# A router of column groups, a shorter routing chain, and ScalarE copying the whole expert output

## The reference

```
scores = sigmoid(x @ router_w)                      # 640 x 16
best group of 4 by the sum of its top 2 of (scores + router_b)
idx    = top 2 experts inside that group;  wts = scores[idx] / sum
rows are sorted by expert, each expert padded to blocks of 128 rows
yb[block] = (silu(xb @ w_gate[e]) * (xb @ w_up[e])) @ w_down[e]
y[token]  = sum over its two rows of wts * yb
```

## Time and profile before

| | us |
|---|---|
| median of 3 runs | 2377.22 |
| lowest and highest of them | 2376.87, 2381.79 |
| profiled execution: time | 2377.54 |
| profiled execution: span from first to last instruction | 2375.8 |

### The profile page before, as it was taken

One profiled execution on the slowest core, in us unless ns is written; L12 is line 12 of the kernel. 1 busy time (PEld: TensorE's weight loads), 2 busy tenths in 40 slices (PEclk: granted clock), 3 DMA queues, 4 the chain that ended last, 5 costly groups with the idle time before them and its releaser, 6 DMA issues. The chain is left out here.

```text
span 2375.8 us, 25720 instructions
## 1 busy us (share of the span) xinstructions
PE 2062.0 (87%) x8680; PEld 1425.4 (60%) x8680; DVE 1159.2 (49%) x1677; ACT 910.7 (38%) x1290; POOL 112.1 (5%) x130
## 2 busy tenths in 40 slices
PE   6869899998479999838999999999999838999974
PEld 2335454454258878727756765874775427788853
DVE  1132323224469999754232423323232248999965
ACT  1021312212368888632211221222221127888853
POOL 0000000000010000011000100100000010000001
PEclk7669999799789999968999999999999968999986
DMA  9967010000689999461211220320210258999933
GB/s 374 409 219 314 22 37 18 19 18 6 241 288 399 399 399 399 175 245 36 80 62 39 75 79 21 101 79 27 71 36 16 77 224 303 398 399 398 399 127 123
DMA packets 169029, 424.88 MB, mean 179 GB/s; under 512 B 10621, under 2 KB 22426, under 8 KB 168986
## 3 DMA queue, kind: packets, MB, share of 16 engines
q1 hardware_dynamic: 152624, 365.52, 41.6%
q0 software_dynamic: 10944, 39.85, 4.5%
q10 hardware_dynamic: 5418, 18.96, 2.0%
HBM read 369.09 MB, written 55.21 MB: 179 GB/s over the span
## 5 line engine op out<-in xcount | busy, mean ns | idle before, releaser
L1768 DVE TENSOR_TENSOR moe_w_lo<-weight_ring,moe_w_hi 128x1024 fp32r<-128x1024 f32 x432 | 520.9, 1222 | 84.5 <-ACT moe_w_hi L1699 71.2
L1699 ACT ACTIVATE moe_w_hi<-weight_ring 128x1024 fp32r<-128x1024 f32 x432 | 456.3, 1060 | 194.3 <-PE ps L1631 125.5
L1631 PE MATMUL ps<-moe_w_hi,moe_rows_t_hi 128*128 128x512 f32 x576 | 232.8, 404 | 5.1 <-DVE moe_rows_t_lo L1773 4.7
L1229 DVE TENSOR_TENSOR ret_w_lo<-weight_ring,ret_w_hi 128x512 fp32r<-128x512 f32 x128 | 95.8, 749 | 286.1 <-ACT ret_w_hi L1165 286.1
L1631 PE MATMUL ps<-moe_w_hi,moe_rows_t_lo 128*128 128x512 f32 x576 | 226.8, 394 | 0.0
L1631 PE MATMUL ps<-moe_w_lo,moe_rows_t_hi 128*128 128x512 f32 x576 | 226.5, 393 | 0.0
L1165 ACT ACTIVATE ret_w_hi<-weight_ring 128x512 fp32r<-128x512 f32 x128 | 80.6, 633 | 309.2 <-PE ps L1042 309.2
L1042 PE MATMUL ps<-ret_w_hi,h_hi 128*128 128x512 f32 x480 | 194.0, 404 | 3.4 <-ACT weight_ring L1169 2.1
L1042 PE MATMUL ps<-ret_w_hi,h_lo 128*128 128x512 f32 x480 | 189.6, 395 | 0.0
L1042 PE MATMUL ps<-ret_w_lo,h_hi 128*128 128x512 f32 x480 | 189.6, 395 | 0.0
L1631 PEld LDWEIGHTS ps<-moe_w_hi,moe_rows_t_hi 128*128 128x128 f32 x576 | 109.3, 190 | 27.7 <-DVE moe_rows_t_lo L1773 5.5
(11 more groups left out here) (283 smaller groups left out, 2967.7 us busy)
## 6 DMA issues: line engine op xcount, KB each, us to landing
weight_ring<-in_moe_w_gate SPq DMA_DIRECT2D x36, 2048.0 KB, 12.7
weight_ring<-in_moe_w_up SPq DMA_DIRECT2D x36, 2048.0 KB, 13.8
weight_ring<-in_moe_w_down SPq DMA_DIRECT2D x36, 2048.0 KB, 12.7
weight_ring<-in_ada_w SPq DMA_DIRECT2D x24, 2048.0 KB, 23.9
weight_ring<-in_ret_w_in SPq DMA_DIRECT2D x12, 2048.0 KB, 8.7
h_normed<-rows_in POOLq DMA_DIRECT2D x36, 512.0 KB, 7.0
rows_out<-h_normed ACTq DMA_DIRECT2D x36, 512.0 KB, 6.2
rows_in<-zero_rows SPq DMA_DIRECT2D x26, 512.0 KB, 7.7
```

Source lines behind the costliest of these rows:

```text
L1229: dve.tensor_tensor(wlo[:, n % BUF, :], win[s][:, k, :], whi[:, n % BUF, :].bitcast(F32), ALU.subtract).then_inc(w_lo, 1)
L1631: mm = pe.matmul(out, lhs, rhs, start=(first and x == 0), stop=(last and x == 2))
L1699: nc.scalar.activation(whi[:, x, :], part(u, w + x), ACT.Identity).then_inc(w_hi, 1)
L1768: dve.tensor_tensor(wlo[:, x, :], part(blk[1], w + x), whi[:, x, :].bitcast(F32), ALU.subtract).then_inc(w_lo, 1)
```

## The change

- Constants: `pick` is 16 columns wide, three small tables go; the router's weights stand in tiles of 32 columns, cleared by POOL at the start, and SP waits for that ahead of their load.
- `norm` gets the router's matmuls, four slices of the width side by side in four groups of 32 output columns; the first half runs when 8 of the 16 shifts are done, the second after the last. `route` sums the four groups with `pick`.
- The routing chain has fewer operations, some of them larger; counts come as a sixth block of the ranks. PE turns two groups of rows ahead of the logits, and has six banks for it.
- In `retention` a mask comes from a table that is there already.
- In `experts` ACT copies both banks of the output, DVE none, and DVE runs `make_hidden` ahead of the last gate split.

```diff
 # norm, PE:
+for q in range(2 if router else 0):
+    pe.wait_ge(shifted, before16 + 8 * (q + 1))
+    for r, (a, n, j) in enumerate(RANGES):
+        for k in range(4):
+            mm = pe.matmul(ps[CG * k:CG * (k + 1), 2 + r, 0:n], c.router[:, 4 * q + k, :],
+                           c.h[:, 4 * q + k, a:a + n], start=(q == 0), stop=(q == 1))
 # setup, SP and POOL:
+sp.wait_ge(cleared, 1)
-sp.dma_start(c.router[:, :, :], ops["router_w"]...)
+sp.dma_start(c.router[:, :, 0:NE], ops["router_w"]...)
+pool.memset(c.router[:, :, :], 0.0).then_inc(cleared, 1)
 # route, PE:
-for r, (a, n, _) in enumerate(RANGES):
-    for k in range(KD):
-        mm = pe.matmul(ps[0:NE, 6 + r, 0:n], c.router[:, k, :], c.h[:, k, a:a + n], ...)
-pe.wait_ge(copied, 2)
-for t in range(NT):
-    mm = pe.transpose(ps[:, 0, t * NE:(t + 1) * NE], logits_t[:, t * P:(t + 1) * P], ...)
 for g in range(2 * NT):
+    if g == 2:
+        pe.wait_ge(copied, 2)
+        for t in range(NT):
+            mm = pe.matmul(ps[:, 6, t * NE:(t + 1) * NE], by_expert[:, t * P:(t + 1) * P], c.base["pick"], ...)
+        mm.then_inc(logits, 1)
     ...  # turn the rows, as before
-pe.matmul(ps[:, 1, 0:NT * NE], c.base["before"], flat, start=True, stop=False)
-for back in range(1, NT):
-    pe.matmul(ps[:, 1, back * NE:NT * NE], c.base["ones"], flat[:, 0:(NT - back) * NE], ...)
-for t in range(NT):
-    mm = pe.matmul(ps[:, 6, 0:NE], c.base["ones"], on[:, t, :], ...)
+pe.matmul(ps[:, RANK_BANK, 0:(NT + 1) * NE], c.base["before"], flat, start=True, stop=False)
+for back in range(1, NT + 1):
+    mm = pe.matmul(ps[:, RANK_BANK, back * NE:(NT + 1) * NE], c.base["ones"], flat[:, 0:(NT + 1 - back) * NE], ...)
 # route, ACT (DVE copies the other 128 columns):
+act.wait_ge(c.routed, layer + 1)
+nc.scalar.copy(by_expert[:, SEQ:T], ps[:, 3, :]).then_inc(copied, 1)
 # route, DVE, pairs of a group:
-11 operations of pair sums and maxima on [P, 20]
+link(dve.tensor_tensor(trio[:, :, 0:2], m[:, :, :, 0], m[:, :, :, 1], ALU.add))
+link(dve.tensor_tensor(high[:, :, :], m[:, :, :, 0], m[:, :, :, 1], ALU.max))
+link(dve.tensor_tensor(trio[:, :, 2], high[:, :, 0], high[:, :, 1], ALU.add))
+link(dve.tensor_reduce(pair[:, :], trio[:, :, :], AX.X, ALU.max))
 # route, DVE, after the ranks:
-4 compares, a copy and 8 operations of a scan over 16 experts, 3 for start, 4 on [P, 80], 2 x 2 for dst
+over_step [P, 80], its sum nb, summand [P, 256], its sum below, start, far, near, far + near [P, 80],
+picked [P, 160], its sum dst
 # experts, ACT:
-nc.scalar.copy(y[:, u, 0:512], ps[:, 5, :]).then_inc(ya, 1)
+nc.scalar.copy(y[:, u, :].rearrange("p (a n) -> p a n", a=2), ps[:, 5:7, :]).then_inc(ya, 1)
 # experts, DVE:
     take_x(after)
-    split(after, GATE, s, 8, (0,))
-    take_y(before, s * UN + (4 + BUF))
-    split(after, GATE, s, 8, (1, 2, 3))
+    split(after, GATE, s, 8, (0, 1, 2))
     make_hidden(now)
+    split(after, GATE, s, 8, (3,))
 # experts: the waits for DVE's half (yv) go from PE's down and ACT's store
 # retention, DVE:
-dve.tensor_tensor(dec[:, 1, LAT - P:LAT], dec[:, 1, LAT - P:LAT], m["trib"], ALU.mult)
+dve.scalar_tensor_tensor(out=dec[:, 1, LAT - P:LAT], in0=c.base["before"], scalar=0.5,
+                         in1=dec[:, 1, LAT - P:LAT], op0=ALU.is_lt, op1=ALU.mult)
```

More of the change, by code:

```diff
@@ L336, in _, with norm @@
                                                      in1=gain, op0=ALU.add, op1=ALU.mult).then_inc(amp, 1)
-def norm(c, call, amp, shift, prefetch=None, parts=None):
+def norm(c, call, amp, shift, prefetch=None, parts=None, router=False):
     nc, ps = c.nc, c.ps
@@ L1337, in route @@
         rows = sb("rows", [P, NT, D])
-        s, gr, msk, o1, o2, on, tmp, past = (sb(n, [P, NT, NE]) for n in
-                                             ("scores", "biased", "masked", "one1", "one2", "both", "tmp", "past"))
-        pair, keep, off = sb("pair", [P, 2, G]), sb("keep", [P, NT, NG]), sb("off", [P, NT, NG])
-        top = sb("top", [P, NT])
[L1342 to L1347, removed]
+        s, gr, msk, far, near = (sb(n, [P, NT, NE]) for n in ("scores", "biased", "masked", "far", "near"))
+        on = sb("both", [P, NT + 1, NE])
+        one, picked = sb("one", [P, TOPK, NT, NE]), sb("picked", [P, TOPK, NT, NE])
+        high, trio, pair = sb("high", [P, G, 2]), sb("trio", [P, G, 3]), sb("pair", [P, G])
+        keep, off = sb("keep", [P, NT, NG]), sb("off", [P, NT, NG])
+        top = sb("top", [P, NT])
+        wsum, dst = sb("wsum", [P, NT]), sb("dst", [P, TOPK, NT])
+        nb, below, start, down = sb("more_blocks", [P, NE]), sb("blocks_below", [P, NE]), sb("start", [P, NE]), sb("countdown", [P, NE])
+        steps, over_step = sb("steps", [P, NT - 1]), sb("over_step", [P, NE, NT - 1])
+        by_expert = sb("by_expert", [P, T])
+        lower, summand, first = sb("lower", [P, NE, NE]), sb("summand", [P, NE, NE]), sb("first_row", [P, NE])
+        cmp, eb, tn, upto = sb("compare", [P, NBLK - NE, NE]), sb("block_e", [P, NBLK]), sb("turns", [P, 2]), sb("blocks_upto", [P, NE])
+        copied, logits, ranks, turned, taken, expd, chain, scattered = sems(
+            nc, st, f"route{layer}", ["copied", "logits", "ranks", "turned", "taken", "exp", "chain", "scattered"])
         with nc.Block(no_gpsimd_drain=True) as block:
@@ L1416, in _ @@
[L1416 to L1424, removed]
@@ new lines, in _ @@
+                link(dve.tensor_reduce(nb[:, :], over_step[:, :, :], AX.X, ALU.add))
+                link(dve.tensor_tensor(summand[:, :, :], lower[:, :, :], nb[:, :].unsqueeze(1).to_broadcast([P, NE, NE]), ALU.mult))
+                link(dve.tensor_reduce(below[:, :], summand[:, :, :], AX.X, ALU.add))
+                link(dve.scalar_tensor_tensor(out=start[:, :], in0=below[:, :], scalar=float(P), in1=first[:, :],
+                                              op0=ALU.mult, op1=ALU.add))
+                link(dve.scalar_tensor_tensor(out=far[:, :, :], in0=rank, scalar=float(P), in1=tiles(start[:, :]),
+                                              op0=ALU.is_ge, op1=ALU.mult))
@@ L1489, in _ @@
                     act.wait_ge(turned, g + 1)
-                    nc.scalar.copy(rows[:, g // 2, 512 * (g % 2):512 * (g % 2 + 1)], ps[:, 2 + g % 4, :]).then_inc(taken, 1)
+                    nc.scalar.copy(rows[:, g // 2, 512 * (g % 2):512 * (g % 2 + 1)], ps[:, TURN_BANKS[g % 6], :]).then_inc(taken, 1)
             @block.gpsimd
```

147 lines of the change are left out of this document (66 added, 81 removed).

## The result

The changed kernel takes 2342.41 us (median of 4 runs, 2341.09 to 2343.77) where the kernel before took 2377.98 (median of 4, 2376.87 to 2381.79): a ratio of 0.9848, 95% interval 0.9831 to 0.9865, so 35.6 us less. The profiled execution took 2341.09, with a span of 2339.4 and a mean granted clock of 0.928.

The account below looks back on a forecast made before the run. Bound by TensorE's wait for `moe_hidden` in each expert block and a route stage where nothing overlaps. Route 25.3 plus experts 7.6 made 32.9 us off 2377.22: 2344 (2337 to 2350; 2332 to 2354 holds 0.8).

Parts of the forecast that it names:

- Router: Route stage: matmuls in four column groups, half before the last shifts, start Exp 6.8 us sooner a layer (6.1 to 7.3).
- the wait for the copies costs nothing: Route: TensorE turns two groups of rows while ScalarE copies and loads its table, both ready at about 617.9.
- Chain: Routing chain on VectorE: fewer operations and shorter ranks save 5.8 us a layer (5.5 to 7.2).
- The ranks: Route: 12 records in place of 20 save 1.83 us at 0.229 a record; at the higher clock up to 3.1.
- Route in all: Router and chain together: 12.6 us a layer, 25.3 for two (23 to 29).
- Expert stage: Experts: 0.18 us a block and 0.9 at the first turn, 3.8 a layer, 7.6 for two (0 to 16).
- The stage's end: End of experts: ScalarE's store waits less, but splits wait for up matmuls and the last copy is longer; costed at nothing.
- The new wait in setup: Setup, SP: wait for POOL's first memset ahead of the router's load and six weight loads; taken as nothing.
- The transfers as the limit: Rival, experts: DMA sets the block, so it can't get shorter; 2352 us, chance 0.15 for no gain there.
- No new stall: Rival, experts: ScalarE's copy is covered, 0.45 us a block saved; 2336 us, chance 0.19.
- Router groups in a row: Rival, router: column groups run one after another, 0.6 us left of 6.8; 2356, chance 0.07 for half worth or less.
- ScalarE's copy as the pace: Rival, experts: ScalarE's two-bank copy paces the block; at 2.1 us it gives 2383, chance 0.04 for slower.

Follow-up runs that it names:

- the last experiment: Changed kernel with hidden rows taken after the first down split and the pick matmuls ahead of the first two groups of row turns: 2325.28 us.

## Why the prediction was right, point by point

- **Router, 6.8 a layer: 6.2.** The groups do run side by side: the second half's 16 records took 2.36 us (forecast 2.3). Off by 0.6: the pick matmuls started 4.7 behind the last shift (forecast 4.6) and took 2.2 up to Exp (forecast 1.7), since they ran at the lower clock throughout, where I had allowed for some of the higher. And "the wait for the copies costs nothing" was only half right: PE was not kept waiting, but the pick matmuls were, behind turns that nobody needs then, 1.06 us as the last experiment shows. That is no miss of the sum, which has the turns in front, but a gain that I didn't see.
- **Chain, 5.8 a layer: 7.0.** Up to the one-hot 1.77 was forecast and 1.77 measured, after the ranks 2.23 and 2.31. The ranks, 1.83, are the mis-sized term: 2.95. I had priced them at the lower clock, since that was the row. But in both profiles of the changed kernel the row turns lasted until shortly before the ranks, 1.12 us of idling in place of 5.25, and the clock stayed up. The bound "at the higher clock up to 3.1" held it. In layer 0 of three other runs with this route the ranks did run at the lower clock, and there the term was 1.71: its price was right for the clock that it assumed, and which of the two it gets the prediction left open.
- **Route in all, 25.3: 26.5** (13.2 and 13.3). Less 0.3, by which the scatter grew.
- **Expert stage, 7.6: 5.5.** The rows came as the text had them: the hole closed, the idle time on VectorE, a new stall of 0.27 for the low half of the hidden rows. The mis-sized term is that stall as a mean: it is 0.27 in one block and 0.40 in the next, so a block gained 0.12 and not 0.18. The first hidden turn came 1.0 earlier behind the load of rows (forecast 0.9), but the block after it was longer by 0.5; the last was shorter by 0.6. The stage's end, costed at nothing, was worth 1 us by the runs with the copy in halves. The new wait in setup does cost nothing: SP issues the router's load at 3.19 us in both kernels.
- **Sum, 32.9.** The route's 26.5 and the experts' 5.5, less 0.3, make 31.7. The rest up to the 36.4 between the two spans, 4.7, is in stretches that the change hardly touches (a cleared tile in setup, one mask operation in retention): setup and modulation 1.7, attention 3.3, retention 0.9, combines and output 0.4, less the 1.7 of layer 0's norm. Setup and attention vary by more than that among the runs with one and the same code there (145.9 to 148.4, 440.1 to 449.4 and once 470.8), so this part is luck as far as is known. The forecast of 2344 is near 2342.4 partly by that, within the range either way.
- **Rivals.** The transfers as the limit: fell. The Trainium skill, "DMA: Bandwidth & Descriptors", section Specifications, gives about 358 GB/s for one core's share; the trace is above that figure, as the run with the hidden rows early kept 399 GB/s for 200 us with a shorter block. The lag grew as forecast: in the changed kernel a gate load took 11.3 us from issue to landing at 691.7 and 14.8 at 927.6, 0.27 a block (forecast 0.3), and nothing waited for it. "No new stall" (2336) didn't come by itself, but moving one operation by one split made more of it than I had priced. Router groups in a row, and ScalarE's copy as the pace: fell; the copy took 1.00 us and held its queue for 0.89.

What stays open: why 0.03 us of the block did not return with the old expert code, whether the shorter attention in both profiles of the changed kernel belongs to the program, and what decides at which clock the route's small matmuls run in layer 0. The shorter chain on VectorE has no run of its own; its gain is read from the rows.

## What to carry to other kernels

When four engines pass a ring of buffers around, look first at the place of the few operations that TensorE waits for: here that was the lever, and relief of VectorE, nearly full as it was, was not. Each fix makes the next of them the late one, so look for that one before stopping: here moving `make_hidden` by one split gave 0.16 us a block (0.12 together with the copy's move), and moving the hidden rows by one split 0.45 more than the changed kernel, until PE had no gap. Before pricing small matmuls at the clock of their row, ask whether the change alters how long TensorE idles ahead of them.

## What the runs showed that I had not expected

- Attention, whose code no kernel here touches, took from 440.1 to 449.4 us in the profiles of eleven of the twelve rows of the table (471 in the other, the experts of before with hidden rows early). DVE and ACT are busy for the same time in all twelve, and the stretch less PE's busy time is 43.1 to 43.6 us: the difference is PE's busy time alone, from 397 us at a granted clock of 0.94 to 406 at 0.92, and 427 at 0.87 in the last. Differences of whole times below some 8 us need the stretches beside them.
- A DMA queue that falls 0.8 us a block further behind is no limit for a loop of 18 blocks with a lead of two.
